# A hybrid encoder layer on one core: x tiles by halves into three PSUM homes, evictions of the up-projection in another order, and part of the state-space products ahead of the states

## The reference

```python
h = rmsnorm(x, norm_mix_g)
z = h @ w_in                       # pooling input, SSM input, q, k, v, forget gates, 3 x 1024 branch gates
gates = sigmoid(z[..., COL_GATE:])
y_a = pool_mixer(u_pool, ...); y_c = fox_attention(q, k, v, ...)
# y_b, the state-space mixer: 32 groups of 16 channels, 64 complex states each
bu = einsum('gpc,blgc->blgp', b_bar, ug);  states = associative_scan(lam_bar, bu)
y_b = glu(gelu(einsum('gcp,blgp->blgc', c_mat, states).real + d_skip * u))
x = x + sum_b(gates_b * (y_b @ w_branch_b)) @ w_out
# ConvFFN: up-projection to 2 x 2816 channels, causal depthwise convolution, gate, down-projection
up = rmsnorm(x, norm_ffn_g) @ w_up
conv = conv_b + sum_j(full[:, j:j + L] * conv_w[j]);  gate, val = split(conv, 2)
x = x + (silu(gate) * val) @ w_down
```

## Time and profile before

| | |
|---|---|
| time, median of 3 runs | 1774.38 us (1773.92 to 1775.85) |
| the profiled execution: its own time | 1773.8 us |
| its span, first to last instruction | 1772.0 us |
| mean granted PE clock over the span, share of full | 0.998 |
| PE busy | 1727.5 us, 97% |
| DVE busy | 1219.3 us, 69% |
| ACT busy | 638.9 us, 36% |
| POOL busy | 677.4 us, 38% |

### The profile page before, as it was taken

The page is one execution under the profiler, slowest core; times in us unless marked ns, Lnnn a source line. Parts: engine busy times, 40 slices in busy tenths (PEclk is TensorE's granted clock), DMA queues, the critical chain, the costliest instruction groups (busy, mean ns, idle before and its releaser), DMA issues.

```text
span 1772.0 us, 31126 instructions
## 1 busy us (share of the span) xinstructions
PE 1727.5 (97%) x12335; PEld 1659.6 (94%) x12335; DVE 1219.3 (69%) x1875; ACT 638.9 (36%) x1209; POOL 677.4 (38%) x473
## 2 busy tenths in 40 slices
PE   7999999999998999999999999999999999999997
PEld 7999999888888889989999998999999999999997
DVE  7788662665665566554564688777777777699685
ACT  5210013555551222241012435444444444534343
POOL 4554433444346667413323334555444554000000
PEclk9999999999999999999999999999999999999999
DMA  8634738766634654366545332222222221998252
GB/s 275 189 124 131 232 107 235 187 165 169 165 108 141 145 107 98 100 191 226 188 134 184 100 96 74 74 74 74 74 74 74 74 74 62 363 343 282 90 191 90
DMA packets 246755, 260.69 MB, mean 147 GB/s; under 512 B 50161, under 2 KB 198365, under 8 KB 246162
## 3 DMA queue, kind: packets, MB, share of 16 engines
q1 hardware_dynamic: 232482, 227.49, 43.1%
q10 hardware_dynamic: 14128, 31.21, 5.0%
HBM read 178.09 MB, written 76.09 MB: 143 GB/s over the span
## 4 chain that ended last, share of the span: by engine, by line
PE 53%; DVE 6%; DMA 4%; issue 3%; ACT 2%; POOL 1%; SPq 0%; POOLq 0%; ACTq 0%; DVEq 0%
PE bank L156 49%; DMA act_raw<-act_scratch 2%; DMA down_raw<-in_w_down 1%; PE bank L1950 1%; DMA gate<-gate_scratch 1%; PE bank L1965 1%; PE bank L1970 1%; DVE merged L2253 1%; DVE prod L2246 0%; PE bank L1935 0%; DVE xt L3081 0%; POOL up_forms L2627 0%; DMA act_scratch<-ffn_act 0%; DVE x L2190 0%; PE bank L1967 0%
## 5 line engine op out<-in xcount | busy, mean ns | idle before, releaser
L156 PE MATMUL bank<-act_hi,w_hi 128*128 128x364 f32 (+1 forms) x1296 | 435.7, 336 | 5.6 <-POOL w_lo L872 1.6
L156 PE MATMUL bank<-act_lo,w_hi 128*128 128x364 f32 (+1 forms) x1296 | 425.6, 328 | 0.0
L156 PE MATMUL bank<-act_hi,w_lo 128*128 128x364 f32 (+1 forms) x1296 | 425.3, 328 | 0.0
L156 PE MATMUL bank<-x_forms,up_forms 128*128 128x272 f32 x1824 | 255.7, 290 | 3.4 <-DVE part_v L3159 3.2
L156 PEld LDWEIGHTS bank<-act_hi,w_hi 128*128 128x128 f32 x1296 | 243.7, 188 | 15.6 <-issue 5.9
L156 PEld LDWEIGHTS bank<-act_lo,w_hi 128*128 128x128 f32 x1296 | 243.7, 188 | 0.1
L156 PEld LDWEIGHTS bank<-x_forms,up_forms 128*128 128x128 f32 x1824 | 239.7, 189 | 4.3 <-DVE up_forms L3143 2.3
L156 PEld LDWEIGHTS bank<-act_hi,w_lo 128*128 128x128 f32 x1296 | 243.2, 188 | 0.0
L156 PE MATMUL bank<-act_form,down_form 128*128 128x272 f32 x1848 | 233.2, 288 | 1.4 <-DVE y_t L3267 0.7
L156 PEld LDWEIGHTS bank<-act_form,down_form 128*128 128x128 f32 x1848 | 231.6, 188 | 2.1 <-DVE y_t L3267 1.3
L2627 POOL TENSOR_TENSOR up_forms<-up_w_raw,up_forms 128x512 fp32r<-128x512 f32 x60 | 88.1, 1469 | 190.6 <-ACT up_forms L2880 190.6
(11 more groups left out here) (376 smaller groups left out, 2964.4 us busy)
## 6 DMA issues: line engine op xcount, KB each, us to landing
down_raw<-in_w_down SPq DMA_DIRECT2D x121, 256.0 KB, 4.5
w_raw<-in_w_in SPq DMA_DIRECT2D x44, 512.0 KB, 4.8
up_w_raw<-in_w_up SPq DMA_DIRECT2D x44, 512.0 KB, 5.0
gate<-gate_scratch ACTq DMA_DIRECT2D x24, 544.0 KB, 3.7
act_scratch<-ffn_act SPq DMA_DIRECT2D x22, 544.0 KB, 4.8
act_raw<-act_scratch SPq DMA_DIRECT2D x44, 272.0 KB, 4.7
gate_scratch<-gate_out ACTq DMA_DIRECT2D x48, 182.0 KB, 2.5
w_raw<-in_w_out SPq DMA_DIRECT2D x14, 512.0 KB, 4.4
```

The source lines that it names most:

```text
L156: mm = pe.matmul(out, w(k), x(k)[:, c0:c0 + cn], start=first and k == ks[0] and n == 0, stop=last and k == ks[-1] and n == 2, skip_group_c ...
```

## The change

It has three parts.

**The entry.** The transposed tiles have three PSUM homes (`home`), and all nine tiles of x have a buffer of their own, so loads wait for nothing but the transposes. High and low parts are made by halves of the channel blocks: ACT copies half a to `xr`, rounds half b to `hh`, and copies half b; DVE rounds half a and makes both low halves. The squares of tiles 0 to 5 stay on ACT but come later, those of tiles 6 to 8 go to DVE after the last tile. ACT makes the diagonal blocks. PE's first groups are cut at four channel blocks. POOL's second weight tile waits for six tiles.

**The state-space layer.** PE waits for `vv` and the Toeplitz tables only, issues the within-chunk products of the sets 0, 2 and 4, and then waits for `sc`.

**The up-projection.** For tile 0, c12 and c21 of the first half are evicted after v and c22 of the second. For tile 1, v and c22 are evicted ahead of one low part. For tiles 2 and 3 (`SETTLED`), v and c22 are evicted ahead of `w_low(j + 1, 2)`, and on ACT `copy_u2` goes ahead of `w_high(j + 1, 2)`.
The diff's pieces are in this order: PE, ACT and DVE in the entry, PE in the state-space layer, ACT and DVE in the up-projection.

```diff
+        home = (0, 1, 2, 0, 1, 0, 1, 0, 1)
+        half_a, half_b = slice(0, KD // 2), slice(KD // 2, KD)
...
-                if j >= 2:
-                    pe.wait_ge(x_lo, j - 1)
+                if j == 2:
+                    pe.wait_ge(g_out, 1)
+                if j > 2:
+                    before = max(b for b in range(j) if home[b] == home[j])
+                    pe.wait_ge(x_lo, before + 1)
+                    pe.wait_ge(x_out, before + 1)
...
-            for q in range(4):
-                group(0, 0, 0, range(2 * q, 2 * q + 2))
+            for q in range(2):
+                group(0, 0, 0, range(4 * q, 4 * q + 4))
                 turn_x(5 + q)
+            turn_x(7)
             pe.wait_ge(x_lo, 6)
-            group(0, 0, 1)
+            group(0, 0, 1, range(4))
+            turn_x(8)
+            group(0, 0, 1, range(4, KD))
             pe.wait_ge(x_lo, 9)
...
-                act.activation(xr[:, :, c0:c0 + cn], by_k[j % 2][:, :, 0:cn], ACT.Copy).then_inc(x_out, 1)
-            act.wait_ge(sq_done, 9)
+                act.activation(xr[:, half_a, cols], x[:, half_a, 0:cn], ACT.Copy).then_inc(x_out_a, 1)
+                act.activation(m.hh[:, half_b, cols], x[:, half_b, 0:cn], ACT.Copy)
+                act.activation(xr[:, half_b, cols], x[:, half_b, 0:cn], ACT.Copy).then_inc(x_out, 1)
+                if j in (4, 5):
+                    square(j - 4)
+            for j in range(2, 6):
+                square(j)
...
-                dve.wait_ge(x_out, j + 1)
-                dve.tensor_copy(hi, x).then_inc(x_hi, 1)
-                dve.wait_ge(x_hi, j + 1)
-                dve.tensor_tensor(m.hl[:, :, c0:c0 + cn], x, hi.bitcast(F32), ALU.subtract).then_inc(x_lo, 1)
+                dve.wait_ge(x_out_a, j + 1)
+                dve.tensor_copy(m.hh[:, half_a, cols], x[:, half_a, 0:cn]).then_inc(x_hi, 1)
+                dve.wait_ge(x_hi, j + 1)
+                dve.tensor_tensor(m.hl[:, half_a, cols], x[:, half_a, 0:cn], m.hh[:, half_a, cols].bitcast(F32), ALU.subtract)
+                dve.wait_ge(x_out, j + 1)
+                dve.tensor_tensor(m.hl[:, half_b, cols], x[:, half_b, 0:cn], m.hh[:, half_b, cols].bitcast(F32), ALU.subtract
+                                  ).then_inc(x_lo, 1)
+            for j in range(6, 9):
...
+                dve.tensor_tensor_reduce(out=dve_sq[0:cn], in0=xtok[j][0:cn], in1=xtok[j][0:cn], scale=1.0, scalar=0.0,
+                                         op0=ALU.mult, op1=ALU.add, accum_out=ss[0:cn, j:j + 1]).then_inc(sq_dve, 1)
...
+        AHEAD_SETS = (0, 2, 4)
...
+            pe.wait_ge(*act_did.at(f"vv{t}"))
+            pe.wait_ge(tm_ld, 256 * (t + 1))
+            for n in AHEAD_SETS:
+                within_chunk(j, *FRAME_SETS[n])
             pe.wait_ge(*dve_did.at(f"sc{t}"))
-            pe.wait_ge(tm_ld, 256 * (t + 1))
...
+SETTLED = 4
...
-EVICTS_FIRST = ("v0", "c22_0", "c11_0", "c12_0", "c21_0", "c11_1", "v1", "c22_1", "c12_1", "c21_1")
+EVICTS_FIRST = ("v0", "c22_0", "c11_0", "c11_1", "v1", "c22_1", "c21_0", "c12_0", "c12_1", "c21_1")
...
-            for i in range(2 if j == 1 else 3):
+            for i in range(2 if j < SETTLED else 3):
                 w_high(j + 1, i)
...
-        plain_low_first(1, 6)
         for n in range(2):
             evict_v(1, n)
             evict_c22(1, n)
+        plain_low_first(1, 6)
         gated(0)
         for j in range(1, LAST):
             w_low(j + 1, 1)
-            w_low(j + 1, 2)
+            if j >= SETTLED:
+                w_low(j + 1, 2)
             if j > 1:
                 for n in range(2):
                     evict_v(j, n)
                     evict_c22(j, n)
+            if j < SETTLED:
+                w_low(j + 1, 2)
```

More of the change, by code:

```diff
@@ L934, in entry_engines @@
         xr = tabs("x_turned", [P, KD, T], start=0)
-        xtok = room("x_tok", [P, 4, D])
+        xroom = room("x_tok", [P, 5, D])
         rows, junk = half("vec_rows", [P, 4, P]), half("x_sq", [P, D])
@@ L1208, in tensor @@
             group(1, 1, 0)
+            group(1, 1, 1, range(4))
             pe.wait_ge(diag_done, 9)
@@ L1212, in tensor @@
             mm.then_inc(bc_done, 1)
-            group(1, 1, 1)
+            group(1, 1, 1, range(4, KD))
             pe.wait_ge(inv_done, 3)
@@ L1312, in scalar @@
                 act.dma_start(m.xt_d[:, 4 * n:4 * n + 4], xr[:, 4 * n:4 * n + 4]).then_inc(xt_st, 16)
+            act.wait_ge(invc_done, 1)
+            for j, (c0, cn) in enumerate(TOK):
+                act.activation(diag[:, c0:c0 + cn], m.ident[:, 0:cn], ACT.Copy, scale=invc[:, j:j + 1]).then_inc(diag_done, 1)
             act.wait_ge(bc_done, 1)
@@ L3010, in scalar @@
             copy_u2(j, 1)
-            for i in range(2 if j == 1 else 3, 6):
+            for i in range(2 if j < SETTLED else 3, 6):
                 w_high(j + 1, i)
@@ L3372, in vector @@
         evict_c22(0, 1)
+        evict_c21(0, 0)
+        evict_c12(0, 0)
         sum_first(1, 1)
```

75 lines of the change are left out of this document (44 added, 31 removed).

## The result

The changed kernel takes 1761.8 us, the median of 4 runs (1760.6 to 1763.0), against 1774.2 us before (1773.9 to 1775.9): a ratio of 0.9933 with a 95% interval from 0.992 to 0.9945, or 12.3 us less (10 to 14). The forecast was 1763.3. The profiled execution took 1760.6 us, with a span of 1758.8.

A forecast was written before the change was run, and what follows sets the result against it. The prediction took PE, busy for 97% of the span, as the bound. Gains of 3.9 (entry), 3.5 (state-space layer) and 3.6 (up-projection) sum to 11.0 us, from 1774.4 to 1763.4; it predicted 1763.3, range 1760.5 to 1767.3.

The forecast's parts named there:

- The entry, 3.9 us forecast: Entry: PE starts the first weight tile's third group at 26.3 in place of 30.3; 3.9 us gained.
- 0.68 or 0.69 us each, 2.06 us a tile: Entry: DVE's three half operations for a tile take 2.06 us in place of 2.44.
- The norm: Entry: diagonal blocks done at 35.7, PE asks for them at 36.3; it just fits, by 0.6 us.
- norm late: Rival, entry: PE waits for the diagonal blocks and 2.2 us are lost, 1765.5 us; chance 0.12.
- The state-space layer, 3.5 us forecast: State-space layer: three sets ahead fill PE's wait for sc; 1.95 us in tile 0, 1.54 in tile 1.
- in tile 0 the wait is 2.53 us: State-space tile 0: of PE's 2.53 us wait for sc, 1.95 us are gained and 0.6 remain.
- Nothing is added: State-space layer: PE asked before as well for what the sets ahead need, so no new wait arises.
- The up-projection, 3.6 us forecast: Up-projection: 3.8 us gained in tile 2 from the wait and lower clock, 0.2 lost in tiles 0 and 1.
- The clock falls elsewhere: Rival, up-projection: the clock falls behind tile 1's two waits for c21, costing 1.65 us, 1765.0 us; chance 0.10.
- The wait moves on: Rival, up-projection tile 3: DVE still late, PE waits 1 to 2 us without the clock, 1765 us; chance 0.07.
- Slower: Rival, up-projection from tile 4 on: the loop stays late and PE waits in each of 18 tiles; 1778.7 at 0.85; chance 0.03.
- The sum: Whole kernel: 3.9 + 3.5 + 3.6 = 11.0 us gained.

The follow-up runs named there:

- act_squares: The changed kernel with all nine squares on ACT and none on DVE; 1764.3 us, ratio 0.9952.
- up_only: The kernel before with only the up-projection's part of the change; 1770.7 us, ratio 0.998.
- settled3: The changed kernel with SETTLED = 3, so v stands ahead of the second low part in up-projection tile 2 but not tile 3; 1762.4 us, ratio 0.9935.
- ssm_only: The kernel before with only the state-space layer's part of the change; 1771.5 us, ratio 0.9991.
- up_tile2_only: The kernel before with only the up-projection's order for tiles 2 and 3, tiles 0 and 1 as before; 1770.8 us, ratio 0.9983.
- two_homes: The changed kernel with two PSUM homes for the entry's input tiles in place of three; 1764.1 us, ratio 0.9942.
- pool_after_sc: The kernel before, with POOL's gain multiplication of weight tile 15 made to wait for DVE's sc of state-space tile 0; 1772.8 us, ratio 0.9998.
- ahead_tile1: The changed kernel with sets ahead of the states in state-space tile 1 only, and POOL's weight tile 15 waiting for tile 0's sc; 1763.0 us, ratio 0.9944.
- whole_tiles: The changed kernel with the entry's halves undone: ACT copies, and DVE rounds and subtracts, whole tiles; 1765.6 us, ratio 0.9959.

## Why the prediction was right

**The entry, 3.9 us forecast.** Halves, homes and norm worked as written; the size was too small by 0.8 us. The step that was mis-sized is "0.68 or 0.69 us each, 2.06 us a tile". It added lengths, where instructions of DVE overlap: from start to start the three are 0.73, 0.61 and 0.59 us, 1.93 a tile, which is 1.0 us less for eight tiles. Part of that was lost again to something that the forecast did not have: a load came late, PE waited 0.73 us for it, and DVE idled 0.47 us at tile 2. The forecast's own sum has a slip besides: 25.1 + 0.9 is 26.0, and it went on with 26.2 and 26.3. The nine tiles were split at 25.6, and the third group started at 25.67. Before it started 4.7 us later, at 30.38, where 30.3 was worked out. The wait for ACT's squares was forecast at 0.9 and came at 0.88.

**The norm.** The blocks were done at 34.7 (forecast 35.7) and asked for at 35.74 (36.3): 1.05 us of slack. DVE's square takes 1.23 us, as I had taken from its rounding, and the first waited out POOL's gain multiplication (25.26 to 27.17), 2.72 us, at no loss. The rival *norm late* did not come; act_squares, where PE waits 1.8 us, shows how near it was. Its price was not well worked out: squares that end at 33.4 or 35.3, asked for at 31.3 with 0.6 us to spare, make PE wait 1.5 or 3.4 us, and 2.2 follows from neither bound.

**The state-space layer, 3.5 us forecast.** The step that failed is "in tile 0 the wait is 2.53 us": that is one execution's number, of a collision that other executions had at 1.67 us or not at all. In tile 1 the wait is 1.5 us in every execution of the old order and gone in the new. "Nothing is added" failed too: each tile pays 0.27 us for the switches of width. The new order took 211.3 us in six executions, collision or not. The old one took 211.8 without it, and 211.8 - 1.54 + 4 x 0.27 = 211.3. With the collision the old order took 213.5 and 214.3, so the new one is worth 0.5 to 2.9 us, 1.5 on the mean of the four unaltered ones, in agreement with the timed 1.6. The forecast of 3.5 was 2 us too high.

**The up-projection, 3.6 us forecast.** Tile 2 gave 3.90 in the trace (forecast 3.8); where the clock does not fall in the old order, the new one gains only 2.35 us (17.43 to 15.08). Tiles 0 and 1 gave 0.1 in up_only and not -0.2: no wait for v was left where I had 0.3, and c21's waits are 0.84 and 0.56 us, smaller than the 1.2 and 0.8 I had worked out. *The clock falls elsewhere* did not come: no execution with the new order shows a fall in the up-projection. *The wait moves on* did not either, because tile 3 was given the new order as well; with the old one 0.5 us would have come back. *Slower*: from matmul 7220 to 9000 all kernels but settled3 took 223.88 us, so the loop of later tiles never lagged.

**The sum.** 11.0 us against 12.3 (10 to 14). By the stretches of all executions the parts are worth 4.9 + 1.5 + 3.8 = 10.2 us on the mean: entry 44.8 (five of the old) less 40.0 (six of the new), though its spread is the clock's in part; tiles 0 to 2 of the up-projection 87.7 (four of the old order) less 83.9. So the sum was right in part by luck: the entry was too small by 0.8 to 1.0 us and the state-space term too large by 2, and these cancel in part. What 12.3 has above 10.2 I can't place; it is within the interval, and attention and down-projection vary by more than that.

**What stays open.** The down-projection takes 417 to 421 us. Cut finer, its spread sits in two places. From matmul 10450 to 11000 it takes 70.1 to 73.7 us. There loads of its weights land late: in ssm_only ACT waited 6.22 us for one (3.67 in before), and PE 2.41 us behind it (not at all in before); some 45 us further on in up_tile2_only DVE waited 1.74 us for another (0.29 in act_squares). In ssm_only and two_homes the clock fell in this place as well.

```profile
1527.96 0.63 ACT L2948 ACTIVATE down_form<-down_raw 128x512 fp32r<-128x512 f32 x1 [6.22 <-DMA down_raw<-in_w_down]
```

```profile
1570.64 0.69 DVE L3233 TENSOR_TENSOR down_raw<-down_raw,down_raw 128x512 f32<-128x512 f32 x1 [1.74 <-DMA down_raw<-in_w_down]
```

From matmul 11700 to 11800 it takes 14.8 us in ten executions and 15.7 in the other four (up_only, pool_after_sc, ahead_tile1, two_homes). Every kernel has the same wait of 1.83 us for `y_t` there, and in these four the lower clock came behind it. The changed kernel, then up_only:

```profile
1673.36 3.71 PE L2866 MATMUL bank<-ident,y_t 128*128 128x128 f32 x32 [1.83 <-DVE y_t L3316]
```

```profile
1684.18 5.38 PE L2818 MATMUL bank<-ident,y_t 128*128 128x128 f32 x32 [1.83 <-DVE y_t L3268]
```

Why the loads come late in some executions, and why the clock falls behind a wait in some and not in others, stays open; no run was made on either.

## What to carry to other kernels

Before a wait is priced, ask what the instruction that PE waited for ran beside: a DVE instruction of several times its usual length beside POOL, with POOL started by a load, is a number of that execution and not of the kernel. Work that PE can do ahead of a late input is an insurance: it costs what its switches cost in every tile, and pays when the input is late. Take an engine's pace from start to start of its instructions, not from their lengths. And before two executions are compared, look at the granted clock in both: here it accounts for some third of what whole_tiles seemed to lose.

## What the runs showed of the hardware

The same wait of PE, 2.13 us, was followed by a lower clock in three executions (1.55 us lost) and not in a fourth; one of 1.83 us near the end was followed by it in four executions (0.9 us lost) and not in ten. In the entry PE's clock reached its upper level for the rest of the entry at 7.8 to 25.7 us, by execution. A DVE instruction with two SBUF inputs and a POOL instruction that reads SBUF shut each other out in either order: POOL's 1.90 us became 2.41 where DVE was first, and DVE's 0.69 became 2.40, or its 0.19 became 1.89, where POOL was. `tensor_tensor_reduce` on 1024 columns from SBUF takes DVE 1.23 us, and needs no longer for 128 rows than for 64 (1.22).
